# The last stage of a PEER decoder layer: combined norm passes on VectorE, and gathered sums that end one round sooner

## The chip, the cores and the metric

The kernel runs on one core of one Trainium2 chip. The metric is the device time of one execution in microseconds. The core has a matrix engine (TensorE), a vector engine (VectorE), an activation engine (ScalarE), a general engine (GpSimd) and an engine that issues transfers (SyncE); each runs its own list of instructions in order, and semaphores tie the lists together. In the profile they are PE (PEld for its weight loads), DVE, ACT, POOL and SP.

## The reference

One decoder layer over 1024 tokens of width 1024, in float32: a mixing part (dilated attention beside a gated delta rule), a layer norm, and then the PEER part with the last layer norm. Only the end concerns the change:

```
experts, gate = product-key retrieval, 8 heads, top 16 of 128*128 experts
act = gelu(x . expert_down[e])
y   = sum over the token's 128 (expert, gate) pairs of gate * act * expert_up[e]
out = layer_norm(ALPHA * x + y, ln2_gain, ln2_bias)      # mean, variance + 1e-5, over 1024
```

## The kernel before

`build_program` runs stages one after another; the change is in the last one, `stage_up`, which starts at about 3265 us of the span. It computes `y` and the last norm. The eight tiles of 128 tokens (`e_y`, 128 x 8 x 1024) are treated in two ways.

Six tiles (`DENSE`) get their sum as a dense product: all 16384 experts in 128 chunks of 128. For a chunk c, SyncE loads three arrays (`load`, L2007): activations `e_araw` and gate weights `e_W`, 384 KB each, and the chunk's 128 rows of `expert_up`, `e_uraw`, 512 KB; they have two buffers each, so `loads` (L2014) waits for `C_lo` of chunk c before it issues chunk c+2. GpSimd multiplies activations by weights (`weigh`, L2062 to L2065). ScalarE rounds both operands to the fast format (`e_uh` L2043, `e_Ch` L2045), and VectorE subtracts to get the remainders (`low`: `e_ul` L2094, then `e_Cl` L2096, which signals `C_lo`). TensorE takes four chunks (G = 4) as one round: `NR` = 32 rounds; in each it fills `BR` = 12 banks (six tiles, two halves of 512), 12 matmuls to a bank, three products for each of four chunks. It starts a round when the round's four `C_lo` are there. Eight PSUM banks exist (`NB`), so a bank is reused once VectorE has added its content to `e_y` (`add`, L2098 to L2106; the first round's form, L2104, also multiplies by ALPHA). ScalarE's and VectorE's results for chunks have eight buffers, two rounds.

Two tiles (`GATHERED`) get their sum row by row: 128 experts to a token, 256 steps in all. For step k GpSimd issues a gather of 128 rows of `expert_up`, 512 KB (`gather`, L2055 to L2059), into one of `NGU` = 8 buffers `e_rows`, once step k-8 has been accumulated; VectorE then does `e_y += coef * row` (`accumulate`, L2109 to L2121). The steps are called rows below, row 0 to row 255.

The order on each engine is written out by hand. GpSimd first weighs chunks 0 to 7, and behind each of chunks 4 to 7 it gathers two rows, 0 to 7. Then for each round r and each q of 0 to 3 it weighs chunk 4(r+2)+q and gathers `per_round[r] // 4` rows, those that lie eight after the round's own (L2073 to L2080). VectorE in round r (`rounds`, L2123) does for each bank b: `add`; as many accumulations as keep the count at `count * (b+1) // 12`; and behind banks 1, 3, 5 and 7 `low` of one chunk of the next round. `per_round` is 8 for all 32 rounds. The rounds from 2 to 29 are a loop.

The last round has no `low`. VectorE accumulates two rows behind each of its first four banks; then for every tile it computes the statistics (`stats_of`, L1972 to L1987: two `bn_stats` over halves, `bn_aggr`, plus epsilon), GpSimd raises to the power -0.5 (L2085), VectorE normalises (`norm`, L1992), and GpSimd multiplies by the gain and adds the bias (`affine`, L1999 and L2001), but for the last tile, where VectorE does so. SyncE stores each tile when it is final (L2032). Gain and bias are loaded into the two `e_uraw` buffers once `C_lo` of the last chunk is there (L2026).

Of the kernel before, what the change touches and what calls it, by code (L numbers as in the profile page):

```python
# [9 lines left out]
ALU = mybir.AluOpType  # L10
# [3 lines left out]
P = 128  # L14
# [3 lines left out]
TT = T // P  # L18
HALF = 512
# [16 lines left out]
ORDER = GATHERED + DENSE  # L36
ND, NG2 = len(DENSE), len(GATHERED)
# [6 lines left out]
START = 16  # L44
# [1892 lines left out]
def stage_up(nc, g):  # L1937
# [3 lines left out]
    NR = NCH // G  # L1941
    NB = 8
    BR = 2 * ND
    NGU = 8
    NU = NG2 * P
    per_round = [NU // NR] * NR
    assert sum(per_round) == NU
    first_up = [sum(per_round[:r]) for r in range(NR)]
    PER_PASS = 2 * per_round[2]
    with ExitStack() as ctx:  # L1950
        def sb(name, shape, dt=F32):
            return ctx.enter_context(nc.sbuf_tensor(name, shape, dt))

        sem = ctx.enter_context(stage_semaphores(nc, "e",
            "y_add rstd normed stats aggr var scaled final ld_A0 ld_A1 ld_u0 ld_u1 C_lo ld_y ld_ln st_out "
            "y_mm u_hi weighted C_hi power y_init scaled_last final_last acc", landed="ld_r0 ld_r1 ld_r2 ld_r3 ld_r4 ld_r5 ld_r6 ld_r7"))
        y = sb("e_y", [P, TT, D])
        uraw = [sb(f"e_uraw{u}", [P, D]) for u in range(2)]
        araw = [sb(f"e_araw{u}", [P, TD]) for u in range(2)]
# [3 lines left out]
        Ch = [sb(f"e_Ch{u}", [P, TD], F32R) for u in range(2 * G)]  # L1963
        Cl = [sb(f"e_Cl{u}", [P, TD], F32R) for u in range(2 * G)]
        rows = [sb(f"e_rows{u}", [P, D]) for u in range(NGU)]
        stats, mv = [sb(f"e_stats{u}", [P, 2, 6]) for u in range(2)], [sb(f"e_mv{u}", [P, 2]) for u in range(2)]
        rstd, power = [sb(f"e_rstd{u}", [P, 1]) for u in range(2)], sb("e_power", [P, 1])
        psy = [ctx.enter_context(nc.psum_tensor(f"e_psy{u}", [P, HALF], F32)) for u in range(NB)]
        block = ctx.enter_context(nc.Block())

        def stats_of(dve, n):

            t, u = ORDER[n], n % 2
            if n >= NG2:
                dve.wait_ge(sem("y_add"), START + BR * (NR - 1) + 2 * (n - NG2) + 2)
            else:
                dve.wait_ge(sem("acc"), START + NU)
            if n >= 2:
                dve.wait_ge(sem("rstd"), START + n - 1)
                dve.wait_ge(sem("normed"), START + n - 1)  # L1980
            for h in range(2):
                ins = nc.vector.bn_stats(stats[u][:, h, :], y[:, t, h * HALF:(h + 1) * HALF])  # L1982
            ins.then_inc(sem("stats"), 1)
            dve.wait_ge(sem("stats"), START + n + 1)
            nc.vector.bn_aggr(mv[u][:], stats[u][:]).then_inc(sem("aggr"), 1)
            dve.wait_ge(sem("aggr"), START + n + 1)
            nc.vector.tensor_scalar(mv[u][:, 1:2], mv[u][:, 1:2], 1e-5, None, ALU.add).then_inc(sem("var"), 1)  # L1987

        def norm(dve, n):
            t, u = ORDER[n], n % 2  # L1990
            dve.wait_ge(sem("rstd"), START + n + 1)
            nc.vector.tensor_scalar(y[:, t, :], y[:, t, :], mv[u][:, 0:1], rstd[u][:, 0:1], ALU.subtract, ALU.mult).then_inc(sem("normed"), 1)  # L1992

        def affine(engine, eng, n, done):

            t = ORDER[n]
            scaled, v = (sem("scaled_last"), 1) if n == TT - 1 else (sem("scaled"), n + 1)
            eng.wait_ge(sem("normed"), START + n + 1)
            engine.tensor_tensor(y[:, t, :], y[:, t, :], uraw[0][:], ALU.mult).then_inc(scaled, 1)  # L1999
            eng.wait_ge(scaled, START + v)  # L2000
            engine.tensor_tensor(y[:, t, :], y[:, t, :], uraw[1][:], ALU.add).then_inc(sem(done), 1)  # L2001

        @block.sync
        def _(sp):
            def load(c, n):  # L2007
                for d, s, name in ((araw, g.act, "A"), (Wt, g.W, "A"), (uraw, g.up, "u")):
                    sp.dma_start(d[n][:], s[bass.ds(c, 1)].rearrange("o p k -> (o p) k")).then_inc(sem(f"ld_{name}{n}"), 16)  # L2009

            load(0, 0)
            load(1, 1)

            def loads(i):  # L2014
                for n in range(2):
                    sp.wait_ge(sem("C_lo"), START + 2 * i + (n + 1))
                    load(2 * i + (n + 2), n)

            loads(0)
            for t in range(TT):  # L2020
                sp.dma_start(y[:, t, :], g.x1[t * P:(t + 1) * P, :]).then_inc(sem("ld_y"), 16)
            with sp.Fori(1, NCH // 2 - 1) as i:
                loads(i)
            sp.wait_ge(sem("C_lo"), START + NCH)
            for d, s in ((uraw[0], g.ln2_gain), (uraw[1], g.ln2_bias)):
                sp.dma_start(d[:], s.partition_broadcast(P)).then_inc(sem("ld_ln"), 16)  # L2026
            for n, t in enumerate(ORDER):
                if n < TT - 1:
                    sp.wait_ge(sem("final"), START + n + 1)
                else:  # L2030
                    sp.wait_ge(sem("final_last"), START + 1)
                sp.dma_start(g.out[t * P:(t + 1) * P, :], y[:, t, :]).then_inc(sem("st_out"), 16)  # L2032
            sp.wait_ge(sem("st_out"), START + 16 * TT)

        @block.scalar
        def _(act):
# [16 lines left out]
        @block.gpsimd  # L2053
        def _(pool):
            def gather(k):  # L2055
                u, n, e = k % NGU, k % NG2, k // NG2
                if k >= NGU:
                    pool.wait_ge(sem("acc"), START + k - NGU + 1)
                nc.gpsimd.indirect_dma_start(out=rows[u][:], out_offset=None, in_=g.up.rearrange("j p d -> (j p) d"),  # L2059
                                             in_offset=bass.IndirectOffsetOnAxis(ap=g.ids[:, n, e:e + 1], axis=0)).then_inc(sem(f"ld_r{u}"), 16)  # L2060

            def weigh(c):  # L2062
                n = c % 2
                pool.wait_ge(sem(f"ld_A{n}"), START + 32 * (c // 2) + 32)
                nc.gpsimd.tensor_tensor(araw[n][:], araw[n][:], Wt[n][:], ALU.mult).then_inc(sem("weighted"), 1)  # L2065

            nc.gpsimd.memset(power[:], -0.5).then_inc(sem("power"), 1)
            for c in range(2 * G):
                weigh(c)
                if c >= G:  # L2070
                    for k in range(NGU // G * (c - G), NGU // G * (c - G + 1)):
                        gather(k)
            for r in range(NR):  # L2073
                for q in range(G):
                    if r + 2 < NR:
                        weigh(G * (r + 2) + q)
                    each = per_round[r] // G
                    for k in range(first_up[r] + each * q, first_up[r] + each * (q + 1)):
                        if k + NGU < NU:
                            gather(k + NGU)  # L2080
            pool.wait_ge(sem("power"), START + 1)
            pool.wait_ge(sem("ld_ln"), START + 32)
            for n in range(TT):
                pool.wait_ge(sem("var"), START + n + 1)
                nc.gpsimd.tensor_tensor(rstd[n % 2][:], mv[n % 2][:, 1:2], power[:], ALU.pow).then_inc(sem("rstd"), 1)  # L2085
                if n >= 1:
                    affine(nc.gpsimd, pool, n - 1, "final")

        @block.vector
        def _(dve):  # L2090
# [54 lines left out]
            rounds(NR - 2, 0, first_up[NR - 2], per_round[NR - 2], prepared=NR - 1)  # L2145
            for b in range(BR):
                add(NR - 1, 1, b)
                if b < per_round[NR - 1] // 2:
                    for k in range(2 * b, 2 * b + 2):
                        accumulate(first_up[NR - 1] + k)  # L2150
                elif b < 3 * NG2:
                    stats_of(dve, b - 2 * NG2)
                elif b < 4 * NG2:
                    norm(dve, b - 3 * NG2)
                if b % 2 == 1 and b >= 4 * NG2 - 1:
                    for n in range(NG2 if b == 4 * NG2 - 1 else NG2 + b // 2, NG2 + b // 2 + 1):
                        stats_of(dve, n)
                        if n > NG2:
                            norm(dve, n - 1)
            norm(dve, TT - 1)  # L2160
            dve.wait_ge(sem("ld_ln"), START + 32)
            affine(nc.vector, dve, TT - 1, "final_last")

        @block.tensor
        def _(pe):
# [134 lines left out]
```

## Time and profile before

| | us |
|---|---|
| median of 3 runs | 4384.47 (4382.84 to 4387.9) |
| the profiled execution | 4384.15 |
| its span in the trace | 4382.4 |
| TensorE's mean granted clock | 0.953 of full |
| PE busy | 3976.0 (91%) |
| DVE busy | 2594.5 (59%) |
| POOL busy | 1706.1 (39%) |
| ACT busy | 1365.2 (31%) |

The shares are averages over seven stages with different limits; only the last stage is changed. All times of rows are from the span's start. "Idle before" is how long the engine had nothing to do before an instruction, and the name after the arrow is what ended that time. Starts of neighbouring VectorE instructions lie a little closer than their durations, since one drains while the next begins.

### The profile page before, as it was taken

Reading aid. Unit: us, or ns where it says so; the run is one execution under the profiler, and the core shown is the slowest. Engines: PE = TensorE matmul, PEld = TensorE weight load, DVE = VectorE, ACT = ScalarE, POOL = GpSimd, SP = SyncE. Lnnn points to the kernel's source line nnn. Section 1 sums busy time; section 2 is a strip of 40 time slices with the busy share of each in tenths; the row PEclk is TensorE's granted clock in tenths of the full one; section 3 lists DMA queues with packets and bytes.
Section 4 is the critical chain, followed back from the end, with each engine's and each line's share of the span. In section 5 each row is a group of like instructions: output and inputs, shape, how many; then the busy total and the mean of one; then the engine's idle time right before and its main releaser. Section 6 shows DMA issues by size and latency. Waiting matters only on the chain. (4 is left out here: it accounts for less than half of the span.)

```text
span 4382.4 us, 61280 instructions
## 1 busy us (share of the span) xinstructions
PE 3976.0 (91%) x21744; PEld 3588.8 (82%) x21744; DVE 2594.5 (59%) x5114; ACT 1365.2 (31%) x2139; POOL 1706.1 (39%) x1159
## 2 busy tenths in 40 slices
PE   9999994977888788989899999989988999999997
PEld 7888884877888667989898999989986888888885
DVE  2154103545555333127787888766457898888888
ACT  2133212643222211113645546355112222222220
POOL 0000004614444003000517752777735555555556
PEclk9999996998999899999999999999999999999998
DMA  3222225632222432233348795978978878888885
GB/s 130 96 95 97 96 81 154 163 84 59 74 74 83 152 111 87 77 102 113 85 147 271 221 303 189 298 230 255 320 263 307 295 284 292 291 286 292 288 288 186
DMA packets 390922, 801.82 MB, mean 183 GB/s; under 512 B 65264, under 2 KB 204400, under 8 KB 389744
## 3 DMA queue, kind: packets, MB, share of 16 engines
q1 hardware_dynamic: 280176, 531.25, 36.2%
q0 software_dynamic: 110592, 268.62, 19.5%
q8 instruction: 85, 1.39, 0.1%
q14 instruction: 69, 0.57, 0.0%
HBM read 623.40 MB, written 154.32 MB: 177 GB/s over the span
## 5 line engine op out<-in xcount | busy, mean ns | idle before, releaser
L1926 PE MATMUL r_psd<-x1h,r_dh 128*128 128x384 f32 x2048 | 704.7, 344 | 28.8 <-DVE r_dl L1723 27.8
L1926 PE MATMUL r_psd<-x1l,r_dh 128*128 128x384 f32 x2048 | 691.4, 338 | 0.0
L1926 PE MATMUL r_psd<-x1h,r_dl 128*128 128x384 f32 x2048 | 690.8, 337 | 0.0
L2171 PE MATMUL e_psy<-e_uh,e_Ch 128*128 128x512 f32 x1536 | 600.1, 391 | 36.0 <-DVE e_Cl L2096 32.1
L1699 POOL DMA_INDIRECT W<-r_put,r_place x256 | 420.7, 1643 | 517.1 <-DVEq L1873 399.3
L2171 PE MATMUL e_psy<-e_ul,e_Ch 128*128 128x512 f32 x1536 | 599.4, 390 | 0.0
L2171 PE MATMUL e_psy<-e_uh,e_Cl 128*128 128x512 f32 x1536 | 599.3, 390 | 0.0
L1741 DVE CUSTOM_DVE_ANT_0 r_rows<-r_rows,r_psx 128x1024 f32<-128x1024 f32 x256 | 305.5, 1215 | 212.3 <-DMA r_rows<-in_down_rows,ids 208.0
L1926 PEld LDWEIGHTS r_psd<-x1h,r_dh 128*128 128x128 f32 x2048 | 391.0, 191 | 31.1 <-DVE r_dl L1723 29.9
L2065 POOL TENSOR_TENSOR e_araw<-e_araw,e_W 128x768 f32<-128x768 f32 x128 | 258.1, 2017 | 403.5 <-DMA e_W<-W 402.7
L1690 POOL DMA_INDIRECT r_rows<-in_down_rows,ids x256 | 274.3, 1071 | 320.5 <-DVE coef L1741 266.8
L2121 DVE SCALAR_TENSOR_TENSOR e_y<-e_rows,coef,e_y 128x1024 f32<-128x1024 f32 x256 | 386.4, 1510 | 9.3 <-DMA e_rows<-in_up,ids 9.1
L1926 PEld LDWEIGHTS r_psd<-x1l,r_dh 128*128 128x128 f32 x2048 | 390.5, 191 | 0.0
L1926 PEld LDWEIGHTS r_psd<-x1h,r_dl 128*128 128x128 f32 x2048 | 389.6, 190 | 0.0
L2043 ACT CAST e_uh<-e_uraw 128x1024 fp32r<-128x1024 f32 x128 | 134.8, 1053 | 795.5 <-DMA e_uraw<-in_up 496.9
L244 PE MATMUL p_ps<-p_xh,p_wh 128*128 128x512 f32 x928 | 362.1, 390 | 10.4 <-DVE p_wl L198 10.4
L2171 PEld LDWEIGHTS e_psy<-e_uh,e_Ch 128*128 128x128 f32 x1536 | 289.6, 189 | 97.3 <-DVE e_Cl L2096 32.9
L244 PE MATMUL p_ps<-p_xl,p_wh 128*128 128x512 f32 x928 | 361.9, 390 | 0.0
L244 PE MATMUL p_ps<-p_xh,p_wl 128*128 128x512 f32 x928 | 361.7, 390 | 0.0
L2059 POOL DMA_INDIRECT e_rows<-in_up,ids x256 | 330.5, 1291 | 58.7 <-issue 46.7
L2171 PEld LDWEIGHTS e_psy<-e_uh,e_Cl 128*128 128x128 f32 x1536 | 289.4, 188 | 60.5
L2171 PEld LDWEIGHTS e_psy<-e_ul,e_Ch 128*128 128x128 f32 x1536 | 289.6, 189 | 60.1
(326 smaller groups left out, 7357.3 us busy)
## 6 DMA issues: line engine op xcount, KB each, us to landing
r_draw<-in_down SPq DMA_DIRECT2D x128, 512.0 KB
e_uraw<-in_up SPq DMA_DIRECT2D x128, 512.0 KB
act<-r_act SPq DMA_DIRECT2D x128, 384.0 KB
e_araw<-act SPq DMA_DIRECT2D x128, 384.0 KB
e_W<-W SPq DMA_DIRECT2D x128, 384.0 KB
W<-r_W SPq DMA_DIRECT2D x32, 1024.0 KB
p_wraw<-in_w_in SPq DMA_DIRECT2D x58, 512.0 KB
hT<-p_out SPq DMA_DIRECT2D x58, 512.0 KB, 2.9
```

The costliest lines, as they stand in the source:

```text
L244: ins = nc.tensor.matmul(ps[u][:, h * HALF:(h + 1) * HALF], a[u][:, k, :], b[:, k, h * HALF:(h + 1) * HALF], start=(k == 0 and n == 0), st ...
L1690: nc.gpsimd.indirect_dma_start(out=rows[u][:], out_offset=None, in_=g.down_rows, in_offset=bass.IndirectOffsetOnAxis(ap=g.ids[:, n, k % P: ...
L1699: nc.gpsimd.indirect_dma_start(out=cells, out_offset=bass.IndirectOffsetOnAxis(ap=place[:, n, e:e + 1], axis=0), in_=put[:, n, e:e + 1], i ...
L1741: nc.vector.tensor_tensor_reduce(out=rows[u][:], in0=rows[u][:], in1=psx[:], scale=1.0, scalar=0.0, op0=ALU.mult, op1=ALU.add, accum_out=d ...
L1926: ins = nc.tensor.matmul(psd[n][:, h, 0:HD], a[c % DEEP][:, k, :], b[:, k, h * HD:(h + 1) * HD], start=(k == 0 and m == 0), stop=(k == KD ...
L2043: nc.scalar.copy(uh[s][:], uraw[n][:]).then_inc(sem("u_hi"), 1)
L2059: nc.gpsimd.indirect_dma_start(out=rows[u][:], out_offset=None, in_=g.up.rearrange("j p d -> (j p) d"), in_offset=bass.IndirectOffsetOnAxi ...
L2065: nc.gpsimd.tensor_tensor(araw[n][:], araw[n][:], Wt[n][:], ALU.mult).then_inc(sem("weighted"), 1)
L2121: nc.vector.scalar_tensor_tensor(o, rows[u][:], scale, o, ALU.mult, ALU.add).then_inc(sem("acc"), 1)
L2171: ins = nc.tensor.matmul(bank[:], a[s][:, t * P:(t + 1) * P], v[s][:, h * HALF:(h + 1) * HALF], start=(q == 0 and m == 0), stop=(q == G - ...
```

## The change

Rows: rounds 0 and 1 accumulate 12 rows each, the last round none, the others 8 as before; GpSimd's gathers follow the same list. Statistics: each half tile has its own `bn_stats`, which for the last tile is computed as soon as that half is added. Norm: instead of subtract and scale on VectorE, and gain and bias on GpSimd, VectorE does two combined passes, `centre`: (y - mean) * gain over the tile, and `finish`: (y * rstd) + bias in two halves. GpSimd keeps the power only. The last tile is stored in two halves. `mv` and `rstd` get one buffer for each tile.

```diff
-    per_round = [NU // NR] * NR
+    per_round = [12, 12] + [8] * (NR - 3) + [0]
...
+        def stats_of(dve, n, h):
             if n >= NG2:
+                dve.wait_ge(sem("y_add"), START + BR * (NR - 1) + 2 * (n - NG2) + h + 1)
+            elif h == 0:
                 dve.wait_ge(sem("acc"), START + NU)
+            nc.vector.bn_stats(stats[n % 2][:, h, :], half(n, h)).then_inc(sem("stats"), 1)
+
+        def centre(dve, n):
+            dve.wait_ge(sem("stats"), START + 2 * n + 2)
+            nc.vector.bn_aggr(mv[n][:], stats[n % 2][:]).then_inc(sem("aggr"), 1)
+            dve.wait_ge(sem("aggr"), START + n + 1)
+            nc.vector.tensor_scalar(mv[n][:, 1:2], mv[n][:, 1:2], 1e-5, None, ALU.add).then_inc(sem("var"), 1)
+            dve.wait_ge(sem("ld_ln"), START + 32)
+            nc.vector.scalar_tensor_tensor(y[:, ORDER[n], :], y[:, ORDER[n], :], mv[n][:, 0:1], uraw[0][:],
+                                           ALU.subtract, ALU.mult).then_inc(sem("centred"), 1)
+
+        def finish(dve, n):
+            dve.wait_ge(sem("rstd"), START + n + 1)
+            dve.wait_ge(sem("centred"), START + n + 1)
             for h in range(2):
+                ins = nc.vector.scalar_tensor_tensor(half(n, h), half(n, h), rstd[n][:, 0:1], uraw[1][:, h * HALF:(h + 1) * HALF],
+                                                     ALU.mult, ALU.add)
...
             for n in range(TT):
                 pool.wait_ge(sem("var"), START + n + 1)
-                nc.gpsimd.tensor_tensor(rstd[n % 2][:], mv[n % 2][:, 1:2], power[:], ALU.pow).then_inc(sem("rstd"), 1)
-                if n >= 1:
-                    affine(nc.gpsimd, pool, n - 1, "final")
+                nc.gpsimd.tensor_tensor(rstd[n][:], mv[n][:, 1:2], power[:], ALU.pow).then_inc(sem("rstd"), 1)
...
             for b in range(BR):
                 add(NR - 1, 1, b)
+                if 1 <= b <= 4:
+                    finish(dve, b - 1)
+                elif b % 2 == 0 and b > 4:
+                    finish(dve, NG2 + b // 2 - 1)
+                if b < NG2:
+                    done = b
+                elif b == NG2:
+                    done = NG2
+                else:
+                    done = NG2 + b // 2 if b % 2 == 1 else None
+                if b == BR - 2:
+                    stats_of(dve, TT - 1, 0)
+                if done is not None:
+                    for h in range(1 if b == BR - 1 else 0, 2):
+                        stats_of(dve, done, h)
+                    centre(dve, done)
+            finish(dve, TT - 1)
```

## Rows read from the trace of the kernel before

**Rows 1.** Waits of the last stage, 3268 to 4350: us in total, times, longest.

```profile
ACT e_uh L2043 <- DMA e_uraw<-in_up: 496.9, 78, 13.1
...
PE e_psy L2171 <- DVE e_Cl L2096: 32.1, 2, 18.9
...
PE e_psy L2171 <- DVE e_y L2104: 3.9, 1, 3.9
```

**Rows 2.** Busy time by window: PE, PEld, DVE, ACT, POOL, then PEclk, DMA share, GB/s.

```profile
3316.00:3318.00 2.00, 2.00 (x6) 1.58 (x5) 2.00 (x4) 0.00 (x0) 0.00 (x0) 0.50 0.94 354
3362.00:3395.00 33.00, 33.00 (x148) 27.31 (x147) 28.06 (x28) 7.25 (x8) 20.56 (x14) 1.00 0.82 294
4317.00:4350.00 33.00, 32.59 (x144) 26.65 (x142) 29.59 (x42) 0.00 (x0) 16.34 (x12) 1.00 0.35 140
4350.00:4382.00 32.00, 0.00 (x0) 0.00 (x0) 24.54 (x23) 0.00 (x0) 25.98 (x14) 0.55 0.26 107
```

**Rows 3.** Instructions in order of time, VectorE, last round: start, us, engine, line.

```profile
4319.70 0.69 DVE L2106 TENSOR_TENSOR e_y<-e_y,e_psy 128x512 f32<-128x512 f32 x1 [0.84 <-PE e_psy L2171]
...
4332.34 1.27 DVE L1982 BATCH_NORM_STATS2 e_stats<-e_y 128x6 f32<-128x512 f32 x2
...
4333.96 0.68 DVE L2106 TENSOR_TENSOR e_y<-e_y,e_psy 128x512 f32<-128x512 f32 x1
...
4336.78 0.81 DVE L1992 TENSOR_SCALAR e_y<-e_y,e_mv,e_rstd 128x1024 f32<-128x1024 f32 x1
```

**Rows 4.** Instructions in order of time, VectorE, rounds 0 and 1.

```profile
3279.50 2.56 DVE L2096 TENSOR_TENSOR e_Cl<-e_araw,e_Ch 128x768 fp32r<-128x768 f32 x1
...
3312.18 1.21 DVE L2094 TENSOR_TENSOR e_ul<-e_uraw,e_uh 128x1024 fp32r<-128x1024 f32 x1
...
3314.18 0.67 DVE L2104 SCALAR_TENSOR_TENSOR e_y<-e_y,e_psy 128x512 f32<-128x512 f32 x1
...
3330.52 1.28 DVE L2121 SCALAR_TENSOR_TENSOR e_y<-e_rows,coef,e_y 128x1024 f32<-128x1024 f32 x1 [3.25 <-DMA e_rows<-in_up,ids]
3331.72 1.22 DVE L2094 TENSOR_TENSOR e_ul<-e_uraw,e_uh 128x1024 fp32r<-128x1024 f32 x1
3332.86 2.56 DVE L2096 TENSOR_TENSOR e_Cl<-e_araw,e_Ch 128x768 fp32r<-128x768 f32 x1
...
3343.23 0.69 DVE L2106 TENSOR_TENSOR e_y<-e_y,e_psy 128x512 f32<-128x512 f32 x1 [1.24 <-PE e_psy L2171]
```

**Rows 5.** Chain that ended last, its end: start us, us, what.

```profile
4368.15 2.67 POOL e_y L2001
...
4371.36 2.83 DVE e_y L1992
...
4374.28 3.18 DVE e_y L1999
...
4377.49 1.23 DVE e_y L2001
```

**Rows 6.** Instructions in order of time, GpSimd, start of the stage.

```profile
3286.33 1.84 POOL L2065 TENSOR_TENSOR e_araw<-e_araw,e_W 128x768 f32<-128x768 f32 x1 [5.08 <-DMA e_W<-W]
...
3321.68 2.22 POOL L2065 TENSOR_TENSOR e_araw<-e_araw,e_W 128x768 f32<-128x768 f32 x1 [7.48 <-DMA e_W<-W]
3324.06 1.98 POOL L2059 DMA_INDIRECT e_rows<-in_up,ids  x1 [0.15 <-issue]
3326.34 0.95 POOL L2059 DMA_INDIRECT e_rows<-in_up,ids  x1 [0.30 <-issue]
...
3340.99 2.11 POOL L2065 TENSOR_TENSOR e_araw<-e_araw,e_W 128x768 f32<-128x768 f32 x1 [2.96 <-DMA e_W<-W]
```

**Rows 7.** DMA issues, end of the stage.

```profile
out<-e_y SPq DMA_DIRECT2D x8, 512.0 KB, 2.6
```

**Rows 8.** All row gathers of the kernel, issue to landing.

```profile
DMA to landing us min/median/max: 4.7/5.8/10.1
```

**Rows 9.** SyncE's queue, in order of time, load of the bias.

```profile
4311.58 0.42 SPq L2026 DMA_DIRECT2D e_uraw<-in_ln_bias  x1
```

More of the change, by code:

```diff
@@ L1954, in stage_up @@
         sem = ctx.enter_context(stage_semaphores(nc, "e",
-            "y_add rstd normed stats aggr var scaled final ld_A0 ld_A1 ld_u0 ld_u1 C_lo ld_y ld_ln st_out "
-            "y_mm u_hi weighted C_hi power y_init scaled_last final_last acc", landed="ld_r0 ld_r1 ld_r2 ld_r3 ld_r4 ld_r5 ld_r6 ld_r7"))
+            "y_add rstd stats aggr var centred final ld_A0 ld_A1 ld_u0 ld_u1 C_lo ld_y ld_ln st_out "
+            "y_mm u_hi weighted C_hi power y_init final_last acc", landed="ld_r0 ld_r1 ld_r2 ld_r3 ld_r4 ld_r5 ld_r6 ld_r7"))
         y = sb("e_y", [P, TT, D])
@@ L1965, in stage_up @@
         rows = [sb(f"e_rows{u}", [P, D]) for u in range(NGU)]
-        stats, mv = [sb(f"e_stats{u}", [P, 2, 6]) for u in range(2)], [sb(f"e_mv{u}", [P, 2]) for u in range(2)]
-        rstd, power = [sb(f"e_rstd{u}", [P, 1]) for u in range(2)], sb("e_power", [P, 1])
+        stats, mv = [sb(f"e_stats{u}", [P, 2, 6]) for u in range(2)], [sb(f"e_mv{n}", [P, 2]) for n in range(TT)]
+        rstd, power = [sb(f"e_rstd{n}", [P, 1]) for n in range(TT)], sb("e_power", [P, 1])
         psy = [ctx.enter_context(nc.psum_tensor(f"e_psy{u}", [P, HALF], F32)) for u in range(NB)]
@@ L1969, in stage_up, with half @@
         block = ctx.enter_context(nc.Block())
-        def stats_of(dve, n):
-            t, u = ORDER[n], n % 2
+        def half(n, h):
+            return y[:, ORDER[n], h * HALF:(h + 1) * HALF]
+        def stats_of(dve, n, h):
             if n >= NG2:
-                dve.wait_ge(sem("y_add"), START + BR * (NR - 1) + 2 * (n - NG2) + 2)
-            else:
+                dve.wait_ge(sem("y_add"), START + BR * (NR - 1) + 2 * (n - NG2) + h + 1)
+            elif h == 0:
                 dve.wait_ge(sem("acc"), START + NU)
-            if n >= 2:
-                dve.wait_ge(sem("rstd"), START + n - 1)
-                dve.wait_ge(sem("normed"), START + n - 1)
-            for h in range(2):
[L1982 to L2001, printed above, removed]
+            nc.vector.bn_stats(stats[n % 2][:, h, :], half(n, h)).then_inc(sem("stats"), 1)
@@ new lines, in finish @@
+        def finish(dve, n):
+            dve.wait_ge(sem("rstd"), START + n + 1)
+            dve.wait_ge(sem("centred"), START + n + 1)
+            for h in range(2):
+                ins = nc.vector.scalar_tensor_tensor(half(n, h), half(n, h), rstd[n][:, 0:1], uraw[1][:, h * HALF:(h + 1) * HALF],
+                                                     ALU.mult, ALU.add)
+                if n == TT - 1:
+                    ins.then_inc(sem("final_last"), 1)
+            if n < TT - 1:
+                ins.then_inc(sem("final"), 1)
@@ L2026, in _ @@
                 sp.dma_start(d[:], s.partition_broadcast(P)).then_inc(sem("ld_ln"), 16)
[L2027 to L2031, printed above, removed]
-                sp.dma_start(g.out[t * P:(t + 1) * P, :], y[:, t, :]).then_inc(sem("st_out"), 16)
-            sp.wait_ge(sem("st_out"), START + 16 * TT)
+            for n, t in enumerate(ORDER[:TT - 1]):
+                sp.wait_ge(sem("final"), START + n + 1)
+                sp.dma_start(g.out[t * P:(t + 1) * P, :], y[:, t, :]).then_inc(sem("st_out"), 16)
+            t = ORDER[TT - 1]
+            for h in range(2):
+                sp.wait_ge(sem("final_last"), START + h + 1)
+                sp.dma_start(g.out[t * P:(t + 1) * P, h * HALF:(h + 1) * HALF], half(TT - 1, h)).then_inc(sem("st_out"), 16)
+            sp.wait_ge(sem("st_out"), START + 16 * (TT + 1))
         @block.scalar
@@ L2081, in _ @@
             pool.wait_ge(sem("power"), START + 1)
-            pool.wait_ge(sem("ld_ln"), START + 32)
             for n in range(TT):
                 pool.wait_ge(sem("var"), START + n + 1)
-                nc.gpsimd.tensor_tensor(rstd[n % 2][:], mv[n % 2][:, 1:2], power[:], ALU.pow).then_inc(sem("rstd"), 1)
-                if n >= 1:
-                    affine(nc.gpsimd, pool, n - 1, "final")
+                nc.gpsimd.tensor_tensor(rstd[n][:], mv[n][:, 1:2], power[:], ALU.pow).then_inc(sem("rstd"), 1)
         @block.vector
@@ L2147, in _ @@
                 add(NR - 1, 1, b)
[L2148 to L2162, printed above, removed]
+                if 1 <= b <= 4:
[15 more added lines that the diff above has]
+            finish(dve, TT - 1)
         @block.tensor
```

## The prediction

> **What bounds the kernel now.** I read the waits of the last stage first. TensorE waits there for almost nothing: 32.1 us in two waits for VectorE's `e_Cl` and 3.9 us in one wait for `y_add`, all near the start; the long waits belong to ScalarE, which is ahead [rows 1]. The windows say the same: in a stretch of the middle TensorE is busy 33.0 of 33 us at full clock, VectorE 28.1 [rows 2]. One bank of `e_psy` takes TensorE 2.72 us: the second bank of round 1 is done as `add` starts at 3343.23, the first of round 31 at 4319.70, 359 banks later [rows 3, 4]. A round is 12 banks, 32.64 us. So the stage is a start, thirty rounds at TensorE's pace, and a tail.
>
> The tail is the stretch in which TensorE does nothing. Its last matmul ends at 4349.6 (32.59 us busy from 4317 [rows 2]) and the span at 4382.4: 32.8 us. The chain shows what is in it: GpSimd's multiply and add with gain and bias, one tile after another, then the last tile's three passes on VectorE, 2.83, 3.18 and 1.23 us, and a store [rows 5].
>
> The start is a loop. For chunk c+2 SyncE waits until `C_lo` of chunk c is written (L2015 on); its load lands; GpSimd weighs it and then issues the next row gathers; VectorE accumulates those rows in its fixed order, and only behind them comes the next `low`, which writes the next `C_lo`. In the trace: `C_lo` of chunk 4 is there at 3314.2; GpSimd weighs chunk 6 at 3321.68 and issues rows 4 and 5 at 3324.06 and 3326.34; VectorE, idle 3.25 us for row 4, accumulates it at 3330.52, and `low` of chunk 7 ends at 3335.42, where TensorE starts round 1 after 13.2 us without work (the 32.1 less the longer wait, 18.9) [rows 1, 4, 6].
>
> **The change, tail.** The last round's rows are gone and every pass is on VectorE. Prices, start to start: `add` 0.60 (0.67 less the 0.07 by which neighbours overlap); the two `bn_stats`, `bn_aggr` and the epsilon 1.62 (4332.34 to 4333.96); a combined pass over a tile 1.20, as the accumulation has the same form (3330.52 to 3331.72), and 0.60 for a half, as `add` of round 0 [rows 3, 4]. Sum: 12 adds 7.2, eight statistics 13.0, eight `centre` 9.6, sixteen halves of `finish` 9.6, together 39.4; with 0.7 for gaps between ordered pairs, 40.1. VectorE starts this with the bank at 4319.70. The first five banks cost it 3.4, 4.6, 4.6, 4.6 and 1.8 us against 2.72 each, so it stays behind TensorE until the end: 4359.8, 10.2 us after the last matmul. PSUM holds eight banks, so this lag doesn't stop TensorE. The last store took 3.7 us of span for 512 KB (4378.7 to 4382.4, landing 2.6 [rows 5, 7]); for a half tile I take 3.3. The tail becomes 13.5 instead of 32.8: **19.3 saved**. GpSimd's power of n is hidden by `centre` of n. The old norm took 0.81 us with GpSimd idle and 2.83 beside its additions [rows 3, 5]; that sharing goes away with them. If VectorE's passes nevertheless ran at such a pace the sum would be some 20 us longer; nothing is left beside them that would do it. The gain and bias loads are issued by 4312, as before, but VectorE now wants them at about 4322 and no longer at the end; the slowest row transfer of the stage took 10.1 us [rows 8, 9], so zero, or at worst 1 us. Behind this wait VectorE's adds are queued. The other new waits (`stats`, `centred`, `rstd` per tile) are VectorE's own or long answered.
>
> **The change, start.** Rounds 0 and 1 now accumulate one row behind each add, where two banks in three had one. This moves every `low` behind later rows. `low` of chunk 7 stood behind row 4, now behind row 7; those of chunks 8 to 11 stood behind rows 8, 9, 11, 12 and now stand behind 13, 15, 17, 19. Rows 14 to 16 are gathered right after chunk 10 is weighed, rows 17 to 19 after chunk 11 (three to a chunk). Chunk 10 is loaded only once `C_lo` of 8 exists. So `C_lo` of 9 waits for a full lap that begins with `C_lo` of 8, and 10 for one that begins with 9. Before, that lag was three chunks.
>
> Prices of a lap: `C_lo` to weighing 5.6 (3335.42 to 3340.99) down to 4.3 (3282.06 to 3286.33) and up to 7.5 (3314.2 to 3321.68); I take 5.0 where little else is in flight. Weighing to first gather 2.4 in the row, 2.1 taken. Gather to landing 4.7 to 5.8 and 6.4 in the row (3324.06 to 3330.5); 5.2 taken. Next gather +1.3 (2.3 in the row). Accumulation 1.2, `low` 2.0 (3312.18 to 3314.18; 3.7 beside GpSimd) [rows 4, 6, 8]. A lap that ends on a second gathered row is 5.0 + 2.1 + 1.3 + 5.2 + 1.2 + 2.0 = **16.8**, on a first one 15.5. Two banks of VectorE work with rows and one `low` are 5.6.
>
> Written out, with C for the end of `low`:
> C4 3316.0 (one row more, +1.8). C5 3321.6. C6 waits for row 5, second gather behind chunk 6; at the loaded prices of the rows (7.4 + 2.4 + 2.3 + 5.8 + 3.2) 3337.1. C7 = +5.6 = 3342.7: round 1 starts 7.3 late.
> C8 needs rows 11 to 13, gathered behind chunk 9, loaded after C7: 5.0 + 2.1 + 5.2, then 6.8 of accumulations, adds and `low`: 3361.8.
> C9 +16.8 = 3378.6. C10 +15.5 = 3394.1. C11 +5.6 = 3399.7: round 2 starts. TensorE was through with round 1 at about 3377.6 and stood 22 us.
> C12 needs rows 23 and 24, behind chunk 13, behind C11: +17.9 = 3417.6. C13 +4.4. C14 one lap after C12, 3434.4. C15 +4.4 = 3438.8: round 3 starts.
> From round 3 on the lag is two and more chunks as before, and VectorE's own 28 us a round catch up. Round 3 started before at 3335.4 + 2.3 + 2 x 32.64 = 3403.0, the 2.3 being what the low clock cost after the pause (3343.23 is 7.8 after the start, two banks are 5.44). So the delay is 35.8. The wait of 3.9 us was enough for that too: from 3316 to 3318 the granted clock was 0.50, the lower of the two levels, 1.2 GHz, after TensorE had stood until 3314.9 [rows 1, 2]. Round 3 now begins behind a pause of about that length, so one such stretch more: +2.0. **37.8 lost**, and none of it comes back, as TensorE sets the pace of all later rounds.
>
> Net +18.5: span 4400.9. The profiled execution took 4384.15, 1.75 over its span, and lies 0.3 under the median 4384.47: **4403 us**.
>
> The Trainium skill (DMA: Bandwidth & Descriptors, section on the anatomy of one DMA) gives one transfer as about 2.0 us plus its bytes over 436 GB/s. By that, as an estimate, 512 KB of rows land in 3.2 and the two operands of the weighing in 3.8 us, each of five laps is 3.2 shorter and the sum is 4387, near (b) below. The least landing in the trace, 4.7 [rows 8], disagrees; no trace here shows a lap with queues this empty.
>
> **Rivals.** (a) *The start absorbs it, the kernel is faster.* If rows were gathered far enough ahead, extra accumulations would sit in VectorE's 4 us of slack a round and only the tail would show: 4384.5 - 19.3 = 4365. For it: the total of rows and bytes is unchanged, eight row buffers exist, and VectorE has slack. Against: the idle time before 3330.52 shows a `low` held by a row already, with a lag of three. It decides if a lap is under 8.2 us (a quarter of a round); the smallest prices give 4.3 + 2.0 + 1.3 + 4.7 + 3.2 = 15.5. 8%.
> (b) *Short laps.* All low prices: C6 2.7 earlier, five later laps 1.3 each, no clock cost: 37.8 - 2.7 - 6.5 - 2.0 = 26.6 lost, net +7.3, 4392, inside 0.2% of before. 12% for within 0.2%.
> (c) *Loaded laps.* At 7.4, 2.4, 2.3 and 6.4, a lap is 21.7; chunks 8 to 15 together 21 later: 4424. Against: less traffic than in the rows. 10%.
> (d) *The tail doesn't shrink.* Last tile as slow as now, +8: 4411, inside the range.
>
> Forecast 70%, including (d). Over 0.2% (8.8 us, about what can be told from no change) slower: 80%; within 12%; faster 8%. The range reaches from below (b), for laps still shorter, to (c): 4386 to 4425.
>
> **What would show it.** TensorE idle before round 2 by some 20 us on `e_Cl`, before round 3 by a few; VectorE's accumulations of rows 14 and 17 idle on DMA, 7 to 10 us each, near 3370 and 3390; last matmul at about 4387; from it to the end 13 to 14 us; no GpSimd pass over `e_y`. Wrong if the last matmul stays near 4350, or if VectorE doesn't wait for rows in round 1.

## The result, and the profile after

The changed kernel takes 4402.27 us (median of 7, 4398.51 to 4406.7) against 4384.47: ratio 1.0043, interval 1.0031 to 1.0056. It is slower by 17.8 us, 0.4%; 4403 had been forecast. The profiled execution has a span of 4404.9.

Its last stage also began later, though nothing before it was changed. GpSimd's first instruction of the stage dates it, here in the kernel before, then after:

```profile
3270.03 0.10 POOL L2067 MEMSET e_power<- 128x1 f32 x1 [18.95 <-POOLq L72]
```

```profile
3274.85 0.10 POOL L2065 MEMSET e_power<- 128x1 f32 x1 [20.76 <-POOLq L72]
```

So of the 22.5 us between the spans, 4.8 lie ahead of the stage. The stage itself, from this instruction to the end of the span, took 1112.4 and takes 1130.1: 17.7 more. Below, "aligned" means that 4.8 are taken off a time of after.

Waits of the last stage, after (total, times, longest):

```profile
DVE e_y L2116 <- DMA e_rows<-in_up,ids: 73.9, 28, 10.3
PE e_psy L2168 <- DVE e_Cl L2091: 61.2, 4, 20.3
```

VectorE's waits for gathered rows are now 73.9 us in 28 times, 54.8 of them up to row 26 (before, 9.1 in three), and TensorE's for `C_lo` 61.2 in four where they were 32.1 in two. TensorE, in order of time, at the starts of rounds 1, 2 and 3:

```profile
3345.66 0.80 PE L2168 MATMUL e_psy<-e_uh,e_Ch 128*128 128x512 f32 x1 [17.75 <-DVE e_Cl L2091]
```

```profile
3402.00 0.79 PE L2168 MATMUL e_psy<-e_uh,e_Ch 128*128 128x512 f32 x1 [20.28 <-DVE e_Cl L2091]
```

```profile
3442.41 0.79 PE L2168 MATMUL e_psy<-e_uh,e_Ch 128*128 128x512 f32 x1 [4.74 <-DVE e_Cl L2091]
```

Round 1 starts after 17.75 us of idle time (13.2 before), round 2 after 20.28 and round 3 after 4.74, both new. VectorE shows on what (row 8, which is still of round 0, then round 1, and in the last line a row of round 2):

```profile
3353.61 1.28 DVE L2116 SCALAR_TENSOR_TENSOR e_y<-e_rows,coef,e_y 128x1024 f32<-128x1024 f32 x1 [7.40 <-DMA e_rows<-in_up,ids]
...
3363.78 1.22 DVE L2089 TENSOR_TENSOR e_ul<-e_uraw,e_uh 128x1024 fp32r<-128x1024 f32 x1
3364.91 0.95 DVE L2091 TENSOR_TENSOR e_Cl<-e_araw,e_Ch 128x768 fp32r<-128x768 f32 x1
...
3376.74 1.28 DVE L2116 SCALAR_TENSOR_TENSOR e_y<-e_rows,coef,e_y 128x1024 f32<-128x1024 f32 x1 [10.28 <-DMA e_rows<-in_up,ids]
...
3379.14 1.29 DVE L2116 SCALAR_TENSOR_TENSOR e_y<-e_rows,coef,e_y 128x1024 f32<-128x1024 f32 x1 [0.52 <-DMA e_rows<-in_up,ids]
3380.35 1.22 DVE L2089 TENSOR_TENSOR e_ul<-e_uraw,e_uh 128x1024 fp32r<-128x1024 f32 x1
3381.48 0.95 DVE L2091 TENSOR_TENSOR e_Cl<-e_araw,e_Ch 128x768 fp32r<-128x768 f32 x1
...
3392.98 1.28 DVE L2116 SCALAR_TENSOR_TENSOR e_y<-e_rows,coef,e_y 128x1024 f32<-128x1024 f32 x1 [8.15 <-DMA e_rows<-in_up,ids]
3394.18 1.22 DVE L2089 TENSOR_TENSOR e_ul<-e_uraw,e_uh 128x1024 fp32r<-128x1024 f32 x1
3395.32 0.95 DVE L2091 TENSOR_TENSOR e_Cl<-e_araw,e_Ch 128x768 fp32r<-128x768 f32 x1
...
3432.79 1.29 DVE L2116 SCALAR_TENSOR_TENSOR e_y<-e_rows,coef,e_y 128x1024 f32<-128x1024 f32 x1 [7.50 <-DMA e_rows<-in_up,ids]
```

GpSimd beside it:

```profile
3370.56 1.84 POOL L2063 TENSOR_TENSOR e_araw<-e_araw,e_W 128x768 f32<-128x768 f32 x1 [13.06 <-DMA e_W<-W]
3372.55 0.96 POOL L2057 DMA_INDIRECT e_rows<-in_up,ids  x1
3373.81 0.96 POOL L2057 DMA_INDIRECT e_rows<-in_up,ids  x1 [0.30 <-issue]
...
3386.81 1.80 POOL L2063 TENSOR_TENSOR e_araw<-e_araw,e_W 128x768 f32<-128x768 f32 x1 [10.80 <-DMA e_W<-W]
3388.75 0.96 POOL L2057 DMA_INDIRECT e_rows<-in_up,ids  x1
```

One lap can be read off. `low` of chunk 8 ends at 3365.86 (L2091). GpSimd, 13.06 us idle, weighs chunk 10 at 3370.56 and issues rows 14 and 15 at 3372.55 and 3373.81; VectorE, 10.28 us idle, takes row 14 at 3376.74 and row 15 at 3379.14, and `low` of chunk 9 ends at 3382.43. The next lap begins there: chunk 11 weighed at 3386.81, row 17 at 3392.98 after 8.15 idle, `low` of 10 ends at 3396.27. The windows show a stage that waits and isn't full:

```profile
3362.00:3395.00 33.00, 18.85 (x82) 14.94 (x80) 14.04 (x16) 3.56 (x4) 9.35 (x8) 0.83 0.50 168
3395.00:3441.00 46.00, 35.67 (x144) 28.94 (x144) 31.73 (x36) 7.23 (x8) 21.76 (x16) 0.86 0.74 260
```

In the same stretch as [rows 2] TensorE is busy 18.9 instead of 33.0 us and the DMA queues move 168 GB/s at a share of 0.50, where they moved 294 at 0.82.

The tail, VectorE's last round:

```profile
4360.76 0.69 DVE L2101 TENSOR_TENSOR e_y<-e_y,e_psy 128x512 f32<-128x512 f32 x1 [0.84 <-PE e_psy L2168]
4361.36 1.28 DVE L1980 BATCH_NORM_STATS2 e_stats<-e_y 128x6 f32<-128x512 f32 x2
...
4362.99 1.28 DVE L1988 SCALAR_TENSOR_TENSOR e_y<-e_y,e_mv,e_uraw 128x1024 f32<-128x1024 f32 x1
4364.18 0.68 DVE L2101 TENSOR_TENSOR e_y<-e_y,e_psy 128x512 f32<-128x512 f32 x1
4364.78 1.41 DVE L1995 SCALAR_TENSOR_TENSOR e_y<-e_y,e_rstd,e_uraw 128x512 f32<-128x512 f32 x2
...
4400.43 1.42 DVE L1995 SCALAR_TENSOR_TENSOR e_y<-e_y,e_rstd,e_uraw 128x512 f32<-128x512 f32 x2 [0.44 <-POOL e_rstd L2082]
```

GpSimd's last power, and the stores:

```profile
4398.87 1.52 POOL L2082 TENSOR_TENSOR e_rstd<-e_mv,e_power 128x1 f32<-128x1 f32 x1 [3.94 <-DVE e_mv L1986]
```

```profile
out<-e_y SPq DMA_DIRECT2D x7, 512.0 KB, 2.6
...
out<-e_y SPq DMA_DIRECT2D x2, 256.0 KB, 2.1
```

The first bank of the last round is added at 4360.76 (4319.70 before), the last pass ends at 4401.85. The last matmul ends at 4390.6, so the tail is 14.3 us where it was 32.8 [rows 2].

### The profile page after: what moved, and what is told of

It is laid out like the page before. It is cut to its first block and busy times, and to the rows that moved or that the text cites. A ratio compares the mean times of both kernels' runs of the same rounds, so it can differ in the third digit from the quotient of the medians.

```text
span 4404.9 us, 61280 instructions
## 1 busy us (share of the span) xinstructions
PE 3987.0 (91%) x21744; PEld 3596.9 (82%) x21744; DVE 2571.5 (58%) x5128; ACT 1365.9 (31%) x2139; POOL 1687.9 (38%) x1145
## 3 DMA queue, kind: packets, MB, share of 16 engines
q1 hardware_dynamic: 280320, 531.25, 36.2%
## 5 line engine op out<-in xcount | busy, mean ns | idle before, releaser
L2168 PE MATMUL e_psy<-e_uh,e_Ch 128*128 128x512 f32 x1536 | 602.8, 392 | 66.0 <-DVE e_Cl L2091 61.2
L2116 DVE SCALAR_TENSOR_TENSOR e_y<-e_rows,coef,e_y 128x1024 f32<-128x1024 f32 x256 | 377.5, 1475 | 74.1 <-DMA e_rows<-in_up,ids 73.9
L2168 PEld LDWEIGHTS e_psy<-e_uh,e_Ch 128*128 128x128 f32 x1536 | 290.9, 189 | 129.6 <-DVE e_Cl L2091 36.9
```

The lines of the kernel that those rows point to most:

```text
L2116: nc.vector.scalar_tensor_tensor(o, rows[u][:], scale, o, ALU.mult, ALU.add).then_inc(sem("acc"), 1)
L2168: ins = nc.tensor.matmul(bank[:], a[s][:, t * P:(t + 1) * P], v[s][:, h * HALF:(h + 1) * HALF], start=(q == 0 and m == 0), stop=(q == G - ...
```

## The experiments

"Stage" is the span less the time of that first GpSimd instruction, from the profiled execution (1112.4 in the kernel before, 1130.1 in the changed one); the ratio, with its interval, compares the runs of both kernels on the same chip and isn't exactly the quotient of the two medians.

| | stage, against before | median us (before) | ratio |
|---|---|---|---|
| changed kernel | +17.7 | 4402.3 (4384.5) | 1.0043 (1.0031 to 1.0056) |
| e1 rows only | +36.9 | 4423.7 (4381.6) | 1.0090 (1.0076 to 1.0105) |
| e2 passes only | -12.1 | 4371.1 (4381.6) | 0.9975 (0.9966 to 0.9985) |
| e3 rows late | +0.2 | 4384.2 (4381.6) | 1.0002 (0.9993 to 1.0011) |
| e4 gathers first | -4.2 | 4378.8 (4381.6) | 0.9992 (0.9983 to 1.0001) |
| e5 low first | +13.2 | 4397.2 (4382.5) | 1.0034 (1.0023 to 1.0045) |
| e6 one round | -1.7 | 4385.1 (4382.5) | 1.0000 (0.9990 to 1.0009) |
| e7 gathers and low first | -7.1 | 4375.1 (4382.5) | 0.9982 (0.9972 to 0.9992) |
| e8 rows late, low first | -4.5 | 4377.5 (4382.5) | 0.9992 (0.9983 to 1.0001) |
| e9 behind the lows | -7.6 | 4375.5 (4382.2) | 0.9982 (0.9973 to 0.9991) |
| e10 split, both orders | -20.1 | 4366.7 (4382.2) | 0.9966 (0.9953 to 0.9978) |
| e11 split, plain | -7.5 | 4377.8 (4382.2) | 0.9987 (0.9978 to 0.9996) |

Each stage time is from a single execution, and it differs from the difference of the medians by up to 5 us. One source of that can be seen: in the kernel before, e2, e3, e6, e9 and e11 every engine has the same order up to the start of round 1, yet round 1 starts 65.4, 62.1, 63.9, 60.5, 64.4 and 64.9 us into the stage, with pauses of 13.21, 8.92, 11.29, 8.85, 11.59 and 12.81 us before it. Differences of a few us between two rows of the table are therefore read from where the stalls sit, not from the time; the ratios of e3, e4, e6 and e8 can't be told from 1.

**e1 and e2: the two halves of the change.**

```diff
 e1, to the kernel before
-    per_round = [NU // NR] * NR
+    per_round = [12, 12] + [8] * (NR - 3) + [0]
...
-                elif b < 3 * NG2:
+                elif 2 * NG2 <= b < 3 * NG2:
...
-                elif b < 4 * NG2:
+                elif 3 * NG2 <= b < 4 * NG2:
 e2, to the changed kernel
-    per_round = [12, 12] + [8] * (NR - 3) + [0]
+    per_round = [NU // NR] * NR
...
+                if b < 2 * NG2:
+                    for k in range(2 * b, 2 * b + 2):
+                        accumulate(first_up[NR - 1] + k)
+                else:      # n = b - 4: finish(n - 1), stats_of(n), centre(n)
```

> The kernel before with only the rows moved (12, 12, then 8, none in the last round); norm and tail as before. Theory (laps: in rounds 0 and 1 each C_lo waits for rows that are gathered behind a chunk which is loaded only after the C_lo before it): round 3 starts some 35 us late, nothing is given back, about 4420 us, TensorE idle some 20 us before round 2 and 5 before round 3. Rival (the loss comes from the new norm passes or their waits): no later last matmul than before, about 4384.

> The changed tail with the rows as before (8 in every round, two behind each of the last round's first four banks; each tile's centre and finish one bank apart from bank 4 on). Theory: start and last matmul as before; VectorE has 40.1 us of last round plus eight rows at 1.2, 49.7 after 4319.7, so the tail is about 24 instead of 32.8 and the time 4375 to 4376. Rival (the passes win nothing unless the rows are gone): 4384.

The rows alone cost 36.9 us of stage, and their tail is as before, 32.6. TensorE in e1, starts of rounds 2 and 3:

```profile
3392.39 0.79 PE L2171 MATMUL e_psy<-e_uh,e_Ch 128*128 128x512 f32 x1 [20.23 <-DVE e_Cl L2096]
```

```profile
3434.71 0.79 PE L2171 MATMUL e_psy<-e_uh,e_Ch 128*128 128x512 f32 x1 [7.35 <-DVE e_Cl L2096]
```

The same stalls as after, with the old norm: the passes have no part in them. The passes alone win 12.1 of stage. Of this 9.1 are the tail, 23.7 instead of 32.8, as expected; the other 3.0 come from a shorter pause before round 1 (13.2 before; TensorE's first row of round 1 in e2 is below), which the passes don't touch. Rows and passes don't simply add (36.9 - 12.1 = 24.8, measured 17.7): at the tail the rows alone save 0.2, the passes alone 9.1, both together 18.5.

```profile
3338.94 0.79 PE L2162 MATMUL e_psy<-e_uh,e_Ch 128*128 128x512 f32 x1 [8.92 <-DVE e_Cl L2091]
```

**e3 and e9: the rows at the other end.** e3 puts the eight rows into round 30, spread over its banks; e9 puts them behind its last four banks.

```diff
-    per_round = [12, 12] + [8] * (NR - 3) + [0]
+    per_round = [8] * (NR - 2) + [16, 0]
 e9 besides, in rounds()
-                done = 0
+                done, late, count = 0, count - 8, 8
...
-                    while done < count * (b + 1) // BR:
+                    while done < count * (b + 1) // BR + late * max(b - 7, 0) // 4:
```

> The changed kernel with rows 8 in rounds 0 to 29, 16 in round 30, none in 31. Theory: start as before, so the 36 us are gone; VectorE's round 30 has 34.5 us of work or more for 32.6, so it enters the last round 2 to 4 us late and the tail is some 17: 4367 to 4370. Rival (moving rows costs wherever they go, as VectorE is short of time): 4385 or more.

e3 missed: nothing won. TensorE started round 31 late (first row), and VectorE and GpSimd in round 30 show why:

```profile
4323.80 0.79 PE L2168 MATMUL e_psy<-e_uh,e_Ch 128*128 128x512 f32 x1 [13.14 <-DVE e_Cl L2091]
```

```profile
4286.44 0.95 DVE L2091 TENSOR_TENSOR e_Cl<-e_araw,e_Ch 128x768 fp32r<-128x768 f32 x1
...
4298.33 1.28 DVE L2116 SCALAR_TENSOR_TENSOR e_y<-e_rows,coef,e_y 128x1024 f32<-128x1024 f32 x1 [7.36 <-DMA e_rows<-in_up,ids]
...
4312.31 1.28 DVE L2116 SCALAR_TENSOR_TENSOR e_y<-e_rows,coef,e_y 128x1024 f32<-128x1024 f32 x1 [8.29 <-DMA e_rows<-in_up,ids]
```

```profile
4292.06 1.84 POOL L2063 TENSOR_TENSOR e_araw<-e_araw,e_W 128x768 f32<-128x768 f32 x1 [7.25 <-DMA e_W<-W]
...
4306.20 1.84 POOL L2063 TENSOR_TENSOR e_araw<-e_araw,e_W 128x768 f32<-128x768 f32 x1 [9.94 <-DMA e_W<-W]
```

Round 30's `low` prepare round 31, and at 16 rows a round they stand behind more rows too. `low` of 124 ends at 4287.4, chunk 126 is weighed at 4292.06, a row gathered behind it lets VectorE go on at 4298.33 after 7.36 us, and `low` of 125 ends at 4301.6. That starts the second lap: chunk 127 is weighed at 4306.20, a row behind it arrives at 4312.31, and only then comes `low` of 126. I had counted the laps at the start only. It was the same mechanism in a place where I had not looked for it, and e9 tests that reading:

> As rows late (8 in every round, 16 in round 30, none in the last), but the eight extra rows of round 30 come two at a time behind its last four banks, after all of its low. Theory (the 13 us stall before round 31 in rows late was two laps of the same kind: low of 125 behind a row gathered after chunk 126, low of 126 behind one gathered after 127): that stall is gone, last matmul as before, VectorE enters the last round some 6 us late, stage 12 to 13 us shorter than before: 4370. Rival (round 30 can't hold 8 more rows in VectorE or the queues): still 4380 or more.

The stall before round 31 is gone in e9: its trace has no idle time of TensorE behind the start of round 1. The stage is 7.6 shorter and not 12 or 13. The first add of the last round comes 11 us later in the stage than in the kernel before, not 6, as VectorE waited for the ninth and tenth row of round 30. GpSimd issues them at 4306.31 and 4308.57, and VectorE starts on them 10.4 and 10.8 us later:

```profile
4316.67 1.29 DVE L2116 SCALAR_TENSOR_TENSOR e_y<-e_rows,coef,e_y 128x1024 f32<-128x1024 f32 x1 [3.56 <-issue]
4319.37 1.28 DVE L2116 SCALAR_TENSOR_TENSOR e_y<-e_rows,coef,e_y 128x1024 f32<-128x1024 f32 x1 [1.41 <-DMA e_rows<-in_up,ids]
```

**e4, e5, e7: cut the lap, leave the rows.** Same rows as the changed kernel (12, 12). e4 exchanges two steps of GpSimd, e5 two of VectorE, e7 does both.

```diff
 e4
-                    if r + 2 < NR:
-                        weigh(G * (r + 2) + q)
                     each = per_round[r] // G
                     for k in range(first_up[r] + each * q, first_up[r] + each * (q + 1)):
                         if k + NGU < NU:
                             gather(k + NGU)
+                    if r + 2 < NR:
+                        weigh(G * (r + 2) + q)
 e5: in rounds(), "if prepared ...: low(...)" moved ahead of "while done ...: accumulate(...)"
```

> The changed kernel, rows 12, 12 as in it, but GpSimd issues a step's gathers ahead of that step's weighing and not behind it. Every row then hangs on a chunk one earlier: the lag between the C_lo that starts a lap and the one that ends it is two chunks where it was one. Theory (the lap, not VectorE's work or the bytes, is the loss): by the same prices C_lo of 11 comes at about 3375.5 where round 1 ends at 3375.7, no stall before rounds 2 and 3, round 3 starts 5 us later than before instead of 35: 4371 to 4373. Rival (8 more rows in two rounds are too much for VectorE or the DMA queues): stall stays, 4400.

> The changed kernel, but VectorE does low ahead of the accumulations behind the same bank. Each C_lo then waits for one row less. Laps, counted again: C_lo of 9 still hangs on 8 (row 14), 10 no longer on 9 but on 8 (row 16), 11 on 9, 12 on 11, 14 on 12. Theory: round 3 starts about 10 us earlier than in the changed kernel, 4391 to 4394. Rival (the lag of rows doesn't matter, only the amount of work): 4402.

> Rows 12, 12 as in the changed kernel, GpSimd's gathers ahead of the weighing and VectorE's low ahead of the accumulations. Theory: as gathers first alone (4371 to 4373), less the one row that C_lo of 7 no longer waits for, 1 to 2 us: 4370. Rival (row transfers issued earlier collide with the chunk loads and delay them): slower than gathers first alone by some us.

e4 wins back 21.9 of stage against the changed kernel, with the same rows, bytes and passes: the order of two steps on an engine that was busy 9 of 33 us in round 1 carries most of the loss. It isn't all that I expected (30): the first add of the last round still comes 14.3 later in the stage than in the kernel before, because the late start of round 1 and a stall of 6.04 us before round 2 stayed:

```profile
3378.96 0.79 PE L2168 MATMUL e_psy<-e_uh,e_Ch 128*128 128x512 f32 x1 [6.04 <-DVE e_Cl L2091]
```

```profile
3339.95 2.46 POOL L2063 TENSOR_TENSOR e_araw<-e_araw,e_W 128x768 f32<-128x768 f32 x1 [7.60 <-DMA e_W<-W]
```

Chunk 8 was weighed at 3339.95, 8.4 us after `low` of 6 had ended, for which I had 5.0: rows 6 to 10 were issued from 3324.9 on and were in flight with its load. Chunk 10 took 6.4 on the same way. Both lie on the way to round 2, one after the other, together 4.8 over my price. e5 wins 4.5, not 10: less than the counted laps. e7 wins 24.8 and was expected at 4370, not 4375; a stall of 5.37 before round 2 stayed in it. Against e4 it is 2.9 better, which the intervals don't separate. Its rival, rows that slow the loads, fits the longer ways of e4 but doesn't turn the sign. No run changed the traffic alone, so the share of that is not shown.

**e6, e8, e11, e10: where rows can go.** e6 uses [8, 12, 8, ..., 12, 0] with the rows spread. e8 is e3 with low first. e11 is e6 with the four extra rows behind the last four banks; e10 is e11 with gathers first and low first.

> The changed kernel with rows 8, 12, 8 and so on, 12 in round 30, none in the last: half the early extra. Laps, counted: C_lo of 10 hangs on 8 and 11 on 9 (lag two), only 12 on 11 (lag one). Theory: a stall of about 1 us before round 2 and about 4 before round 3, with the clock some 9 us lost at the start, 1 us more in the tail: 4376. Rival (loss in proportion to rows moved): half of 36 lost, 4384.

> The candidate: rows 8, ..., 16, 0 and low ahead of the accumulations. With 8 rows in round 0, C_lo of 7 then waits for row 3, not row 4, so for no row that is gathered behind chunk 6. Theory: round 1 starts about 8 us earlier than in the kernel before (near 3327 instead of 3335), the rest as with the rows late: 4360 to 4363. Rival (the wait before round 1 is the load of the chunks itself): no gain over rows late, 4367 to 4370.

> Four extra rows in round 1 and four in round 30, one behind each of the last four banks, engines' orders otherwise as in the changed kernel. Theory: low of chunks 8 to 11 stand behind rows 8, 9, 11, 12 as before, no lap before round 2; low of 12 and 13 behind rows 20 and 21, gathered after chunk 13 (three to a chunk in round 1), which is loaded after C_lo of 11: one lap, about 17 us after 11, then 14 one lap after 12: a stall of 4 to 6 before round 3. VectorE's slack of 4 us takes the late rows, so the tail stays near 15: 4371. Rival (placing behind the low alone is enough): no stall, 4364.

> The candidate: four extra rows behind the last banks of rounds 1 and 30, GpSimd's gathers ahead of the weighing, VectorE's low ahead of the accumulations. Theory: no lap of lag one anywhere, so no stall after round 1's; that one some 2 us shorter; tail 14 to 15: stage 18 to 20 us shorter than before, 4362 to 4366. Rival (gathers issued earlier slow the chunk loads, as they did in gathers first, where loading and weighing took 8 us): a stall of some us before round 2 or 3, 4370.

e6 had stalls of 5.75, 5.86 and 0.69 us before rounds 2, 3 and 31, where 1, 4 and none were expected, and so won nothing; its 4385 is what the rival, a loss in proportion to the rows, had said. e11 decides against the rival: it has the same number of rows in every round, only placed behind the last banks, and 4.71 us of stalls behind round 1's start instead of 12.3. e8 missed by 17: a stall of 5.79 before round 31 was left, and round 1 started 2 us earlier in the stage, not 8, which is no more than the spread named above. `low` of 7 now waited for ScalarE's rounding, which waited for the chunk's load, the rival:

```profile
3335.34 1.22 DVE L2089 TENSOR_TENSOR e_ul<-e_uraw,e_uh 128x1024 fp32r<-128x1024 f32 x1 [3.49 <-ACT e_uh L2041]
```

e11 has the one stall that was counted, before round 3, but not the time: 4377.8 for an expected 4371. Its tail is 19.2 us where some 15 were expected. The last matmul ends 6.2 later in the stage than in the kernel before, and the first add of the last round comes 11.1 later, as VectorE waits for late rows there too.

```profile
3416.33 0.52 PE L2168 MATMUL e_psy<-e_uh,e_Ch 128*128 128x512 f32 x1 [4.71 <-DVE e_Cl L2091]
```

e10 has none behind round 1's, whose idle time is 11.94, a tail of 16.1, and the lowest time of all, with ratio 0.9966 (its interval overlaps those of e2, e7 and e9, so that it is the fastest isn't shown): 15.4 us faster than the kernel before, where the change was 17.8 slower, each against the runs of before beside it:

```profile
3332.76 0.79 PE L2168 MATMUL e_psy<-e_uh,e_Ch 128*128 128x512 f32 x1 [11.94 <-DVE e_Cl L2091]
```

## Why the prediction was right

By its steps, C being the end of `low` of that chunk, aligned:

| | C4 | C6 | C7 | C8 | C9 | C10 | C11 | C12 | C14 | C15 |
|---|---|---|---|---|---|---|---|---|---|---|
| forecast | 3316.0 | 3337.1 | 3342.7 | 3361.8 | 3378.6 | 3394.1 | 3399.7 | 3417.6 | 3434.4 | 3438.8 |
| measured | 3316.5 | 3335.2 | 3340.8 | 3361.0 | 3377.6 | 3391.5 | 3397.0 | 3415.5 | 3433.1 | 3437.5 |

- *The start.* 37.8 forecast. The first add of the last round moved from 4319.70 to 4360.76, aligned by 36.2; e1, which holds this part alone, has +36.9. The lap from C8 to C9 took 16.6 (forecast 16.8): 4.7 from `C_lo` to weighing (5.0), 2.0 to the first gather (2.1), 1.3 to the second (1.3), 5.3 to its landing (5.2), 1.2 and 2.1. The one from C9 to C10 took 13.8 instead of 15.5; there the row landed in 4.2. By the fit that the Trainium skill (DMA: Bandwidth & Descriptors, the anatomy of one DMA) gives for transfers issued by GpSimd it would be an estimated 3.2: with the queues half empty the trace came nearer to that than before, but no gather of this profile landed faster than 4.2. The prediction took that fit for SyncE's loads too, for which that section doesn't give it. The other steps were longer than forecast: C7 to C8 20.3 (19.1), C11 to C12 18.4 (17.9), C12 to C14 17.6 (16.8). Together with C6, 1.9 early, they partly cancel, so the sum is better than its terms.
- *The low clock after a pause.* 2.0 forecast behind the pause before round 3. Round 3 started 34.7 late, the last round 36.2 late: 1.5.
- *The tail.* 19.3 forecast, 18.5 measured. VectorE took 41.1 us from 4360.76 on, not 40.1: a pair of halves of `finish` costs 1.33 start to start and not 1.20, and the last one waited 0.44 for GpSimd. The half store ended 3.1 after the last pass (3.3). So rival (d) is out.
- *Rival (a)*, that the start absorbs the rows, is out: the lap was 14 to 17 us where it had to be under 8.2. e4 shows what brings the kernel nearer to it: not more slack, but another order. Even so, its start still lost 14.3. *(b) and (c)*, shorter and fuller laps: of the two laps from C8 to C10, one cost what I took for it and the other 13.8, where the lowest prices add up to 14.2; no lap reached the 21.7 of (c). *The chance of 80% for slower* rested on a dependence that could be read in the code and of which one wait was visible before.
- What the forecast didn't contain: the time ahead of the stage. Among the thirteen profiles here it is between 3264.8 and 3279.1, with the same instructions. That the profiled span of after lies 4 us over the forecast is owed to this and not to a step. The stage grew by 17.7 where 18.5 was forecast: 1.6 less lost at the start, 0.8 less saved at the tail. That the median comes within 1 us is in part luck, since the pause before round 1 alone varied by more than 4 us between kernels of the same order.

## What to carry to other kernels

Before work is moved to where an engine has slack, write down for each moved step what it stands in front of in its engine's order, and follow that around until it comes back to the same engine. If a buffer's release, a load, a product and a wait close into a loop, what counts is how many items the loop lags: at a lag of one the price is the latency of a whole lap, here 13.8 to 16.6 us with VectorE busy 14 of 33 and the queues at half. Work that feeds nothing is better placed behind the last step that releases a buffer, at either end of a loop; it isn't free there, as the tails of e9 (26.0 us) and e11 (19.2) against 14.3 show.

## What the runs showed of the hardware that I had not expected

GpSimd's power of a 128 x 1 tile took 550 ns in the kernel before (mean of eight) and takes 1514 now, where `centre`, a VectorE pass with two SBUF operands, runs beside it (row at 4398.87); `centre` itself kept its 1.28 us. It goes with the passes and not with the rows: e1 has 550, e2 1514. Each of the eight powers started 0.2 us after its `centre` and ended 0.4 after it, as if it had waited for the end; spans of GpSimd are rough in this profile, but VectorE's last `finish` did wait 0.44 us for the last power. What held it, no run shows.

The length of a single pause doesn't tell whether the granted clock falls behind it (the seventh figure behind the bounds, PEclk). In e11 TensorE stood 2.31 us until 3323.8, and the clock went to 0.50, 1.2 GHz; in e8 it stood 2.34 until 3317.6 and in e5 3.42 until 3315.0, and the clock stayed at 1.00, 2.4 GHz. Pauses of 1.56 and 0.94 in e10 left it at 1.00 as well. One row each of e11, e8 and e5:

```profile
3325.00:3327.00 2.00, 2.00 (x6) 1.52 (x6) 2.00 (x3) 0.00 (x0) 0.00 (x0) 0.50 0.79 263
...
3318.00:3320.00 2.00, 2.00 (x11) 1.61 (x10) 0.29 (x1) 0.00 (x0) 0.94 (x1) 1.00 1.02 378
...
3315.00:3317.00 2.00, 2.00 (x9) 1.66 (x10) 2.00 (x3) 0.00 (x0) 0.17 (x1) 1.00 0.78 252
```

When it falls differs too. In e11 TensorE stood 4.71 until 3416.3, and the clock was still 1.00 in the last 2 us of the pause and fell only while matmuls ran again:

```profile
3414.00:3416.00 2.00, 0.00 (x0) 0.00 (x0) 2.00 (x3) 0.00 (x0) 0.00 (x0) 1.00 0.98 369
3416.00:3418.00 2.00, 1.67 (x5) 1.35 (x6) 2.00 (x4) 0.00 (x0) 0.64 (x1) 0.67 0.86 266
3418.00:3420.00 2.00, 2.00 (x6) 1.58 (x5) 2.00 (x3) 1.33 (x2) 1.85 (x2) 0.50 0.95 346
3420.00:3422.00 2.00, 2.00 (x10) 1.58 (x9) 2.00 (x3) 0.55 (x1) 1.70 (x2) 0.98 0.73 279
```

In the changed kernel, behind the pause of 4.74 before round 3, it was down to 0.50 before the first matmul at 3442.41 already:

```profile
3442.00:3444.00 2.00, 1.59 (x4) 1.31 (x5) 2.00 (x4) 0.00 (x0) 0.00 (x0) 0.50 0.97 378
```

So the 2 us that the prediction put on the pause before round 3 was a choice that came true, not something that the length of a pause guarantees.
